# One-pass norms with late gain and bias, single last experts and a halved store in a Mamba/Hyena/PEER backbone

## The reference

```python
def layer_norm(x, g, b):
    xf = x.astype(jnp.float32)
    mu = jnp.mean(xf, axis=-1, keepdims=True)
    var = jnp.mean(jnp.square(xf - mu), axis=-1, keepdims=True)
    return ((xf - mu) * lax.rsqrt(var + LN_EPS) * g.astype(jnp.float32) + b.astype(jnp.float32)).astype(x.dtype)
...
        x = layer_norm(DEEPNORM_ALPHA * x + g1 * y_lat, ln_g[i, 0], ln_b[i, 0])
        x = layer_norm(DEEPNORM_ALPHA * x + g2 * peer_ffn(x * (1 + sc2) + sh2, *peer_w), ln_g[i, 1], ln_b[i, 1])
...
        act = jax.nn.gelu(jnp.einsum('td,thkd->thk', tb, u_tab[ib]).astype(f32), approximate=False)
        return jnp.einsum('thk,thkd->td', (gb * act).astype(tb.dtype), v_tab[ib])
```

## Time and profile before

| | before |
|---|---|
| runs, us | 2027.61, 2026.54, 2025.71; median 2026.54 |
| profiled execution, us | 2028.78 |
| its span in the profile, us | 2026.9 |
| TensorE clock granted, of full | 0.963 |
| busy, share of the span | PE 85%, VectorE 74%, ScalarE 30%, GpSimd 24% |
| chain that ended last | PE 39%, DMA 33%, VectorE 20%, nothing shown ("issue") 3% |
| longest part of that chain | expert row transfers 32%, then expert matmuls (L939) 17% |
| moved | 668.13 MB, 330 GB/s over the span; GpSimd's transfers 536.90 MB |

### The profile page before, as it was taken

How to read it: one execution, slowest core, us unless ns; L and a number is a source line. 1 busy time by engine, 2 the same in 40 slices (tenths; PEclk the granted TensorE clock), 3 DMA queues, 4 the chain that set the end, 5 groups by cost and what they waited for, 6 DMA issues and landing times.

```text
span 2026.9 us, 18032 instructions
## 1 busy us (share of the span) xinstructions
PE 1717.1 (85%) x5374; PEld 965.0 (48%) x5374; DVE 1503.3 (74%) x3525; ACT 601.8 (30%) x1424; POOL 483.5 (24%) x516
## 2 busy tenths in 40 slices
PE   5989999969799877898899899968888877877776
PEld 5777478755354432333343578555444422332232
DVE  7889995787577767888887586666677777876755
ACT  2555652512222223323322111012232222322221
POOL 0000000013233333333333000023333333333331
PEclk9999999979999999899999899989999999899999
DMA  8333116759999999999999675359999999999996
GB/s 331 125 114 137 42 63 233 284 222 420 420 419 420 417 412 411 351 413 411 410 403 419 254 271 207 146 223 391 419 418 414 414 417 416 383 420 420 416 411 266
DMA packets 94473, 668.13 MB, mean 330 GB/s; under 512 B 11271, under 2 KB 11560, under 8 KB 14504
## 3 DMA queue, kind: packets, MB, share of 16 engines
q0 software_dynamic: 73728, 536.90, 64.9%
q1 hardware_dynamic: 20648, 130.08, 16.7%
HBM read 665.82 MB, written 1.11 MB: 329 GB/s over the span
## 4 chain that ended last, share of the span: by engine, by line
PE 39%; DMA 33%; DVE 20%; issue 3%; ACT 2%; PEldq 0%; POOL 0%; PEld 0%; DVEq 0%; SPq 0%; POOLq 0%; ACTq 0%
DMA expert_rows<-in_p_uv,chosen_experts 32%; PE bank L939 17%; DVE dot_products L1956 5%; PE bank L1013 4%; PE bank L907 4%; DVE conv_work_or_state L1648 3%; PE bank L740 2%; PE bank L828 2%; PE bank L787 2%; DVE modulation_products L1473 1%; PE bank L1089 1%; PE bank L798 1%; DVE weights_lo L537 1%; ACT weight_diagonal L1341 1%; PE bank L1053 1%
## 5 line engine op out<-in xcount | busy, mean ns | idle before, releaser
L939 PE MATMUL bank<-expert_rows,weight_diagonal 128*128 128x512 f32 x2048 | 973.6, 619 | 209.4 <-ACT weight_diagonal L1341 208.4
L1956 DVE SCALAR_TENSOR_TENSOR dot_products<-expert_rows,bank 128x1024 f32<-128x1024 f32 x512 | 624.8, 1220 | 318.6 <-DMA expert_rows<-in_p_uv,chosen_experts 310.2
L1118 POOL DMA_INDIRECT expert_rows<-in_p_uv,chosen_experts x512 | 483.3, 944 | 1515.0 <-PE bank L939 828.8
L939 PEld LDWEIGHTS bank<-expert_rows,weight_diagonal 128*128 128x128 f32 x2048 | 385.2, 196 | 738.2 <-issue 393.7
L1332 ACT ACTIVATE expert_gelu<-expert_dots 128x2 f32<-128x2 f32 x256 | 51.9, 203 | 688.8 <-DVE dot_products L1956 688.5
L1341 ACT ACTIVATE weight_diagonal<-constants,expert_weights 128x128 f32<-128x128 f32 x512 | 177.6, 394 | 242.2 <-DVE expert_weights L1888 240.6
L907 PE MATMUL bank<-t_T,weight_block 128*128 128x256 f32 x448 | 108.8, 389 | 10.2 <-DVE t_T L1498 10.2
L907 PEld LDWEIGHTS bank<-t_T,weight_block 128*128 128x128 f32 x448 | 87.7, 196 | 43.8 <-issue 33.7
L740 PE MATMUL bank<-mixer_input_T_hi,weights_hi 128*128 128x512 f32 (+1 forms) x192 | 75.5, 393 | 24.3 <-DVE mixer_input_T_lo L1549 14.8
L1013 PE MATMUL bank<-hyena_input_T,hyena_weight_block 128*128 128x256 f32 x384 | 86.3, 385 | 0.7 <-DVE hyena_input_T L1498 0.7
L1648 DVE SCALAR_TENSOR_TENSOR conv_work_or_state<-conv_work_or_state,channel_vectors 128x252 f32<-128x252 f32 (+1 forms) x192 | 82.4, 430 | 4.4
(11 more groups left out here) (260 smaller groups left out, 1897.0 us busy)
## 6 DMA issues: line engine op xcount, KB each, us to landing
weight_block<-in_ada_rows SPq DMA_DIRECT2D x24, 1024.0 KB, 4.8
weight_block<-in_m_in_blocks SPq DMA_DIRECT2D x20, 1024.0 KB, 4.8
weight_block<-in_wq_blocks SPq DMA_DIRECT2D x16, 1024.0 KB, 9.5
hyena_weight_block<-in_ada_rows SPq DMA_DIRECT2D x16, 1024.0 KB, 6.0
hyena_weight_block<-in_h_in_blocks SPq DMA_DIRECT2D x12, 1024.0 KB, 7.0
weight_block<-in_m_out_blocks SPq DMA_DIRECT2D x8, 1024.0 KB, 6.8
expert_rows<-in_p_uv,chosen_experts POOLq DMA_INDIRECT x512, 12.4
hyena_weight_block<-in_h_out_blocks SPq DMA_DIRECT2D x4, 1024.0 KB, 6.9
```

The source lines that it names most:

```text
L939: last = mm(ps[b][:, :], dg[n % DIAG][:, :], uv[slot][:, D + h * 512:D + (h + 1) * 512], start=(r == 0 and k == 0), stop=end)
L1118: pool.indirect_dma_start(uv[slot][:, :], None, A[f"p_uv{l}"], bass.IndirectOffsetOnAxis(ap=chosen[:, s_, k:k + 1], axis=0)).then_inc(uv_l ...
L1956: stt(prod[:, :], uv[slot][:, 0:D], 1.0, rows_t, ALU.mult, ALU.mult, accum_out=dots[:, s_, k + j:k + j + 1]).then_inc(sem("dots_done"), 1)
```

## The change

- **One-pass norm.** For three of the four norms, `ln_norm` replaces `ln_finish`: after the reciprocal of the root, one instruction subtracts the mean and multiplies by the reciprocal, both columns of one number per token. The gain and bias rows aren't needed for it.
- **Folded rows.** What goes to the matmuls must still have gain and bias. `fold_gain(l, pair)` puts them into the columns: shift += scale * bias, scale *= gain, three VectorE instructions of 128 x 8. Gain and bias of all channels are appended as 64 columns to `channel_vectors` (482 to 546), and there is a new tile `folded_bias` of 128 x 8. The folds stand behind the modulation bias in the Mamba mixer's tail, at step 14 of PEER 0 (with two biases that stood behind the stage), and before the norm of Hyena's output.
- **Rows finished later.** `ln_apply` multiplies `x_residual` by the gain row and adds the bias row, two instructions of 128 x 1024, once the modulated copy has been made: at steps 3 and 4 (k = 2) of both PEER stages, and after blocks 0 and 1 of Hyena. The transfers of the rows wait for `norms_applied` instead; those for (1, 0) stand behind the last Hyena weights.
- **Last norm.** `ln_last` (both tiles) keeps the two passes, the second in two halves of 512 columns. The store is four transfers of 256 KB, each waiting for its half (`out_halves`).
- **Last two experts.** In step 15 of both layers, experts 14 and 15 are taken one by one through dot product, gelu, gates and diagonal (`turns`).

```diff
+    def turns(s_):
+        if s_ < PSTEPS - 1:
+            return [(k, PAIR) for k in range(0, TOPK, PAIR)]
+        return [(k, PAIR) for k in range(0, TOPK - PAIR, PAIR)] + [(k, 1) for k in range(TOPK - PAIR, TOPK)]
...
         def ln_rows(l, j):
-            sp.wait_ge(sem("layer_norms_done"), TT * (2 * l + j))
+            sp.wait_ge(sem("norms_applied"), TT * (2 * l + j))
...
-        ln_rows(1, 0)
         weights(HYENA_RING, 8, hyena_ring)
         sp.dma_start(hc[:], A["hyena_constants"]).then_inc(sem("hyena_in"), 16)
         weights(8, len(hyena_ring.blocks), hyena_ring)
+        ln_rows(1, 0)
...
-        sp.wait_ge(sem("layer_norms_done"), TT * 4 - 1)
-        sp.dma_start(out[0, 0:P, :], xres[:, 0, :]).then_inc(sem("out_stored"), 16)
-        sp.wait_ge(sem("layer_norms_done"), TT * 4)
-        sp.dma_start(out[0, P:T, :], xres[:, 1, :]).then_inc(sem("out_stored"), 16)
+        for t in range(TT):
+            for h in range(2):
+                sp.wait_ge(sem("out_halves"), 2 * t + h + 1)
+                sp.dma_start(out[0, t * P:(t + 1) * P, h * 512:(h + 1) * 512], xres[:, t, h * 512:(h + 1) * 512]).then_inc(sem("out_stored"), 16)
...
+        def fold_gain(l, pair):
+            o = KD * (2 * l + pair - 1)
+            shift, scale = ada[l][:, 3 * pair, :], ada[l][:, 3 * pair + 1, :]
+            after(step(tt(folded[:, :], scale, vec[:, V_LNB + o:V_LNB + o + KD], ALU.mult)))
+            step(tt(shift, shift, folded[:, :], ALU.add))
+            after(step(tt(scale, scale, vec[:, V_LNG + o:V_LNG + o + KD], ALU.mult)))
...
-        def ln_finish(l, j, t):
-            n = step(stt(xres[:, t, :], xres[:, t, :], small[:, t, 12:13], lnb[:, 0, :], ALU.subtract, ALU.mult))
+        def ln_norm(l, j, t):
             dve.wait_ge(sem("ln_root"), TT * (2 * l + j) + t + 1)
             m = step(V.reciprocal(small[:, t, 16:17], small[:, t, 15:16]))
             after(m)
-            stt(xres[:, t, :], xres[:, t, :], small[:, t, 16:17], lnb[:, 1, :], ALU.mult, ALU.add).then_inc(sem("layer_norms_done"), 1)
+            ts(xres[:, t, :], xres[:, t, :], small[:, t, 12:13], small[:, t, 16:17], ALU.subtract, ALU.mult).then_inc(sem("layer_norms_done"), 1)
+        def ln_apply(l, j, t):
+            ln_rows(l, j)
+            n = step(tt(xres[:, t, :], xres[:, t, :], lnb[:, 0, :], ALU.mult))
+            after(n)
+            tt(xres[:, t, :], xres[:, t, :], lnb[:, 1, :], ALU.add).then_inc(sem("norms_applied"), 1)
...
-                    weigh_experts(s_, k)
+                    weigh_experts(s_, k, width)
+                    if s_ in (3, 4) and k == 2:
+                        ln_apply(l, 0, s_ - 3)
+                    if l == 0 and s_ == PSTEPS - 2 and k == 2:
+                        for part in range(2):
+                            modulation_bias(1, part)
+                        fold_gain(1, 0)
...
             hyena_block(i)
+            if i < TT:
+                ln_apply(0, 1, i)
```

More of the change, by code:

```diff
@@ L516, in unit, with turn @@
         return n, n % UVR, 16 * (n // UVR + 1)
+    def turns(s_):
+        if s_ < PSTEPS - 1:
+            return [(k, PAIR) for k in range(0, TOPK, PAIR)]
+        return [(k, PAIR) for k in range(0, TOPK - PAIR, PAIR)] + [(k, 1) for k in range(TOPK - PAIR, TOPK)]
+    def turn(l, s_, k):
+        return unit(l, s_, k)[0] // PAIR + l * (PAIR - 1) + (k % PAIR if s_ == PSTEPS - 1 else 0)
     def half_block(name, q):
@@ L1327, in gate_exp, with gelu, diagonals @@
                 f(gexp[:, s_, :], selv[:, s_, :], ACT.Exp, accum_out=gsum[:, s_, 0:1]).then_inc(sem("gate_exp"), 1)
-            def gelu(s_, k):
+            def gelu(s_, k, width):
                 n = unit(l, s_, k)[0]
-                act.wait_ge(sem("dots_done"), n + PAIR)
-                f(gel[:, s_, k:k + PAIR], dots[:, s_, k:k + PAIR], ACT.Gelu).then_inc(sem("gelu_done"), 1)
-            def diagonals(s_, k0):
-                n0 = unit(l, s_, k0)[0]
-                act.wait_ge(sem("expert_weights"), n0 // PAIR + 1)
-                for k in range(k0, k0 + PAIR):
+                act.wait_ge(sem("dots_done"), n + width)
+                f(gel[:, s_, k:k + width], dots[:, s_, k:k + width], ACT.Gelu).then_inc(sem("gelu_done"), 1)
+            def diagonals(s_, k0, width):
+                act.wait_ge(sem("expert_weights"), turn(l, s_, k0) + 1)
+                for k in range(k0, k0 + width):
                     n = unit(l, s_, k)[0]
@@ L1374, in peer @@
             for s_ in range(PSTEPS):
-                for k in range(0, TOPK, PAIR):
-                    gelu(s_, k)
-                    diagonals(s_, k)
+                for k, width in turns(s_):
+                    gelu(s_, k, width)
+                    diagonals(s_, k, width)
                     if s_ == 0 and k == 0:
@@ L1802, in ln_finish, with ln_last @@
             after(m)
-            stt(xres[:, t, :], xres[:, t, :], small[:, t, 16:17], lnb[:, 1, :], ALU.mult, ALU.add).then_inc(sem("layer_norms_done"), 1)
+            ts(xres[:, t, :], xres[:, t, :], small[:, t, 12:13], small[:, t, 16:17], ALU.subtract, ALU.mult).then_inc(sem("layer_norms_done"), 1)
[4 more added lines that the diff above has]
+            tt(xres[:, t, :], xres[:, t, :], lnb[:, 1, :], ALU.add).then_inc(sem("norms_applied"), 1)
+            dve.wait_ge(sem("norms_applied"), TT * (2 * l + j) + t + 1)
+        def ln_last(t):
+            ln_rows(1, 1)
+            n = step(stt(xres[:, t, :], xres[:, t, :], small[:, t, 12:13], lnb[:, 0, :], ALU.subtract, ALU.mult))
+            dve.wait_ge(sem("ln_root"), TT * 3 + t + 1)
+            m = step(V.reciprocal(small[:, t, 16:17], small[:, t, 15:16]))
+            after(m)
+            for h in range(2):
+                c = slice(h * 512, (h + 1) * 512)
+                stt(xres[:, t, c], xres[:, t, c], small[:, t, 16:17], lnb[:, 1, c], ALU.mult, ALU.add).then_inc(sem("out_halves"), 1)
         for k in range(4, INNER // P):
@@ L1929, in filters @@
                     filter_reciprocal(m)
-                if second and k >= 6:
+                if second and k >= 6 and k % PAIR == 0:
                     filter_spectrum(m, (k - 6) // 2)
@@ L1949, in peer @@
                     gates_of(0)
-                for k in range(0, TOPK, PAIR):
-                    for j in range(PAIR):
+                for k, width in turns(s_):
+                    for j in range(width):
                         n, slot, loaded = unit(l, s_, k + j)
@@ L1977, in peer @@
                     if s_ == PH + 1 and k == 2:
-                        ln_finish(l, 1, 0)
+                        if l:
+                            ln_last(0)
+                        else:
+                            ln_norm(l, 1, 0)
                     if l == 0 and s_ >= PH:
@@ L1987, in _ @@
         peer(0, [("mout", j) for j in range(4)])
-        for part in range(2):
-            modulation_bias(1, part)
         modulate_tile(("hhT",), hhT, 1, 0, 0)
```

34 lines of the change are left out of this document (20 added, 14 removed).

## The result

| | before | after |
|---|---|---|
| median, us | 2026.64 (2025.71 to 2027.61, 4 runs) | 2004.44 (1993.75 to 2009.19, 4 runs) |
| ratio | | 0.9886, 95% interval 0.9867 to 0.9905 |
| profiled execution; its span, us | 2028.78; 2026.9 | 2009.19; 2007.4 |
| chain that ended last | PE 39%, DMA 33%, VectorE 20% | PE 39%, DMA 31%, VectorE 21% |

The kernel became 1.1% faster, 22 us, where I had forecast 5.3 us and a range down to 2018.5. The forecast was wrong by size: 17 us are in none of the terms of my sum. The four runs lie 15 us apart, those of before 2 us; over the later sets of 13 to 27 runs the kernel before spreads by 9 to 12 us too.

A forecast was written before the change was run, and what follows sets the result against it. Transfers were taken to bound most of the expert stages, so gains count only at stage starts and ends. The terms, with +0.08 for the larger column table, sum to -5.30 us: median 2021.2 us, range 2018.5 to 2024.8 (8 in 10).

The forecast's parts named there:

- The bound: Transfers limit most of the two expert stages, at 420 GB/s; shorter VectorE work gains only where a stage begins or ends.
- rival (d): Shifted buffer addresses put expert rows on a 256 B multiple; some 13 us per cent of transfer speed, 2008 or 1987; chance 0.07.
- Norm before PEER 0: Norm before layer 0's experts, tile 0: one pass of 0.80 us starting 0.83 us earlier, -1.31 us; tile 1: 0.
- Norm before Hyena: Norm before the second mixer, tile 1: only the shorter pass counts, 1.28 to 0.80 us, -0.49 us.
- rival (c): TensorE's rise to full clock doesn't move with its earlier restart at three norms: 1.5 us lost, 2022.7; chance 0.15.
- Norm before PEER 1: Norm before layer 1's experts, tile 1: -1.31 us; other bound -0.5 if GpSimd's issue delays the pass; tile 0: 0.
- Finishing passes: Late gain and bias, 2.44 us: hidden by gaps and queue in expert stages, by 2.50 us idling after Hyena blocks; 0.
- Step 9: Layer 0, 848 to 852 us, second pair's tile-0 norm: one pass instead of two, -0.50 us, between -1.7 and 0.
- Last two experts: Taken one by one, four records instead of eight remain after the last diagonal: -1.70 us in layer 1, 0 in layer 0.
- Final store: Last pass and store by halves, the second half having 256 KB of 512 KB: -0.55 us, bounds 0 and -0.65.
- Fold: Three small instructions after the modulation bias, on VectorE's chain through the mixer's tail: +0.48 us, 0 if a wait swallows it.
- the line of 2022.5: Faster means below 2022.5 us, as a measurement can tell 0.2%, or 4.05 us, from no change; chance of faster 0.63.

The follow-up runs named there:

- e4: Kernel before with a 64 B unused tile, so that the row buffers begin 32 B beyond a multiple of 256 B: 2025.67 us, ratio 1.0003.
- e1: Kernel before with one unused 32 B tile behind layer_norm_small, so that the row buffers begin on a multiple of 256 B: 2007.08 us, ratio 0.9906.
- e5: Kernel before with unused tiles around the expert-row and Hyena-weight slots only, these two rings beginning on multiples of 256 B: 2007.27 us, ratio 0.9912.
- e13: Changed kernel, rows 224 B beyond a multiple of 256 B, layer 0 keys issued ahead of filter constants and hidden rows: 2020.23 us.
- e14: Changed kernel with rows 224 B beyond a multiple of 256 B, run again on the same chip as e13: 2020.05 us.
- e15: Changed kernel with all rings on multiples of 256 B, last four experts one by one, layer 0 keys issued first: 1999.58 us.
- e2: Changed kernel with a 224 B unused tile behind folded_bias, giving the rows their old offset of 224 B: 2020.26 us, ratio 0.9969.
- e3: Kernel before with a 160 B unused tile, so that the row buffers begin 128 B beyond a multiple of 256 B: 2022.23 us, ratio 0.9987.
- e10: Changed kernel, rows at 224 B, gain and bias of x_residual left out at steps 3 and 4 of both expert stages: 2019.81 us, ratio 0.9965.
- e11: Changed kernel, rows at 224 B, each finishing step in the expert stages done three times: 2024.3 us, ratio 0.9990.
- e12: Changed kernel with all rings on multiples of 256 B and the last four experts one by one, not two: 1998.75 us, ratio 0.9878.
- e7: Changed kernel as it stands, run again on another chip: 1995.13 us, ratio 0.9856.
- e8: Changed kernel with unused tiles that put the weight blocks' ring, x_residual and ln_gain_bias on multiples of 256 B too: 2001.65 us, ratio 0.9877.

## Why the prediction was wrong, point by point

- **The bound.** Right as to where transfers limit, but I took their speed for given. A gain "added up there, place by place" leaves out a thing that acts everywhere. That was seen as rival (d) and given 0.07. The step that failed: the sum put the buffers' addresses at nothing, on the evidence that "other buffers at other offsets are filled at similar speed". Those buffers, the rows and the weight blocks, lay at 224 and at 32 B, and e4 shows that 32 costs as much as 224. I had compared two misaligned buffers. In its place the runs show 19.2 us (e1, e5: 19.3) from transfers that are 1.7% faster. Rival (d)'s price was right: at 13 us for each per cent 1.7% gives 22 us; the 2.7% that it took from the beats was too much.
- **Norm before PEER 0** (-1.31). The pass took 0.81 for 0.80, and TensorE started 2.85 - 1.54 = 1.31 sooner. What is late next was not asked: the scores came 13.56 us behind the variance in the profile of after, 13.20 before, as TensorE waited for the keys; in e13 and e14 they came 1.05 us sooner, in e15, where the clock rose sooner, 2.1 (423.56 to 434.63). So the term is anything from -2.1 to +0.4, and -1.1 where the keys are there in time.
- **Norm before Hyena** (-0.49): 3.34 - 2.88 = 0.46. In the profile of after the clock took back more than that: VectorE takes up the first Hyena block's conv inputs 17.27 us behind the variance (1134.79 to 1152.06), before 16.64, and the clock rose to full 11.7 us behind it, before 9.9. That is rival (c), in one place. In e2 the conv inputs came 0.30 us sooner than before, and in e3 and e4, whose norms are those of before, 0.50 and 1.06 later. So a term of 0.46 is below what one trace tells of this stage.
- **Norm before PEER 1** (-1.31): 2.80 - 1.49 = 1.31, and the first dot product has all of it (also in e2, 5.66 us behind the variance). The bound of -0.5, a pass waiting behind GpSimd, didn't come, though GpSimd was first. The Trainium skill (SBUF - State Buffer, Who interferes with whom) would have the later one fully blocked, if the pass runs in the two-port mode that it speaks of; here the later one ran at its own 0.81 us and the earlier one was stretched, from the 0.94 us of the next. The trace doesn't agree, as far as GpSimd's spans, which are rough, can tell.
- **Finishing passes** (0 in the expert stages): confirmed by e10 as far as the medians can tell, and the cover has an end by e11. Between the Hyena blocks the margin was as small as reckoned; VectorE in after, the next block's first instruction:

```profile
1159.04 0.48 DVE L2057 SCALAR_TENSOR_TENSOR hyena_v_T<-hyena_conv_in,channel_vectors,hyena_v_T 128x255 f32<-128x255 f32 x1 [0.18 <-ACT hyena_conv_in L1146]
...
1165.95 0.48 DVE L2057 SCALAR_TENSOR_TENSOR hyena_v_T<-hyena_conv_in,channel_vectors,hyena_v_T 128x255 f32<-128x255 f32 x1
```

Of 2.50 us of idling 0.18 are left before block 1 and none before block 2, which still begins 6.91 us behind it, as before.
- **Step 9** (-0.50). The stretch 840 to 860 moved 301 GB/s before at a share of 0.82, and 307 at 0.83 in e2: 6 / 420 of 20 us, 0.3. But e3 and e4, whose norm is that of before, moved 292 and 329 there, and e10, which has the new one, 291: what this term was worth can't be read from one trace.
- **Last two experts** (-1.70): 1.45. The step that was off: the pile before the last expert. TensorE started experts 12 and 13 at 1991.20 and ran 16 records in a row, 7.13 us, so the last four did not start when their diagonal was ready (1996.04). e12 gets the rest.
- **Final store** (-0.55): 0.4. The two halves of the pass take 1.42 us together, not 1.28, a cost of 0.14 that I didn't count.
- **Fold** (+0.48): exactly that. VectorE in after, the bias instruction and the one that used to follow it after 0.20 us:

```profile
363.61 0.17 DVE L1493 SCALAR_TENSOR_TENSOR modulation_columns<-modulation_columns,channel_vectors 128x8 f32<-128x8 f32 x1
...
364.29 0.17 DVE L1752 RECIPROCAL rms<-rms 128x2 f32<-128x2 f32 x1
```

0.68 us apart now.
- **Sum.** With the sizes read above -1.1 - 0.46 - 1.31 - 0.3 - 1.45 - 0.4 + 0.48 + 0.08 = -4.5 (the second and the fourth are under the traces' scatter, the last was never measured), and e2's interval is 3.9 to 8.7. The sum is right for the change without its address, within what can be measured; that it comes within 1 us of e2's 6.0 is in part luck.
- **Range and chances.** A range of 2018.5 to 2024.8 left (d) out as the smallest of the cases, though it was the one with the largest effect by far. Faster (0.63) was right, for the most part by a cause that had been given 0.07; without it, e2's 2020.26 is below the line of 2022.5 too.

## What to carry to other kernels

A change that adds or enlarges a buffer also moves all that lie behind it; before its instructions are priced, look at which transfer destinations change their offset within 256 B, above all where transfers bound a stage. Test it with an unused tile on the old kernel, which is a one-line edit and here was worth three times the change's own instructions. A gain at a stage's start is only as large as the time to the next thing that is late, so name that thing too.

## What the runs showed of the hardware

- Packets of 8 KB into a buffer on a multiple of 256 B took 309 ns (e1, 480 to 700 us); 224 B off it most took 313 or 320 ns: 428 against 420 GB/s over 40 us. 32 B off is as bad as 224 B off; 128 B off is a little better.
- Kernels with aligned rows spread by 6 to 15 us in 4 to 6 runs, the kernel before by 9 to 12 us in 13 to 27. A part of it can be seen. In the profile of after (2009.19 us) and in that of the same kernel in e7 (1993.9 us), 1000 to 1040 us:

```profile
1000.00:1040.00 40.00, 37.89 (x88) 16.38 (x88) 31.79 (x74) 12.63 (x29) 14.12 (x15) 1.00 1.02 377
```

```profile
1000.00:1040.00 40.00, 39.30 (x92) 17.05 (x91) 36.03 (x82) 13.25 (x31) 15.93 (x17) 1.00 1.01 427
```

In the profile of after most 8 KB packets took about 352 ns, not 309, from 910 to 940 and from some 995 to 1065 us. These 100 us at 377 to 386 GB/s, not 427, are an estimate of 10 to 12 of the 15 us between the two executions. Such stretches are in the traces of after, e1, e8, e12 and e15, 20 to 100 us in all, not in those of e5 and e7, and in no trace of a kernel whose rows are off 256 B. What makes them was not tried.
- A tensor-by-two-columns pass over 128 x 1024 took 0.81 us, the two-tensor form 1.28. Beside the one GpSimd's issue took 1.21 us, beside two of the other 1.81, and in the mean 0.94.
